# RMSNorm statistics issued chunk by chunk inside the projections, and the FFN-down split around the next tile's front

## What is computed

```
h = rmsnorm(x, g_pre1)
z = h @ w_in                    # 512 columns for S5, 256 for pooling, 256 memory queries
y_ssm = gelu(S5 scan(z[:512]));  y_ssm *= sigmoid(y_ssm @ w_glu + b_glu)
y_pool = per-group linear(trailing means 2/4/8/16 minus the frame)
y_mem = attention of 4 heads into 256 memory tokens
gates = sigmoid(h @ w_gate + b_gate)
merged = gates0*(y_ssm @ w_br_ssm) + gates1*(y_pool @ w_br_pool) + gates2*(y_mem @ w_br_mem)
x = x + rmsnorm(merged @ w_out, g_post1)
h2 = rmsnorm(x, g_pre2)
a, g = split(h2 @ w_ffn_up);  f = (gelu(causal depthwise conv3(a)) * g) @ w_ffn_down
x = x + rmsnorm(f, g_post2)
```

## Time and profile before

| | us |
|---|---|
| median of 2 runs (3299.61 and 3336.57) | 3318.09 |
| the profiled execution's own time | 3302.41 |
| span of its slowest core, core 6 | 3301.0 |
| spans of the 8 cores | 3282.2 to 3301.0 |
| TensorE (matmul) busy on core 6 | 1810.6 (55%) |
| TensorE weight loads | 1355.1 (41%) |
| VectorE busy | 1449.1 (44%) |
| ScalarE busy | 962.0 (29%) |
| GpSimd busy | 686.0 (21%) |

### The profile page before, as it was taken

One profiled execution on the slowest core, in us unless ns is written; L12 is line 12 of the kernel. 1 busy time (PEld: TensorE's weight loads), 2 busy tenths in 40 slices (PEclk: granted clock), 3 DMA queues, 4 the chain that ended last, 5 costly groups with the idle time before them and its releaser, 6 DMA issues.

```text
span 3301.0 us, 52796 instructions; the slowest of 8 cores (3282.2 to 3301.0 us)
## 1 busy us (share of the span) xinstructions
PE 1810.6 (55%) x16066; PEld 1355.1 (41%) x16066; DVE 1449.1 (44%) x2761; ACT 962.0 (29%) x2215; POOL 686.0 (21%) x2374
## 2 busy tenths in 40 slices
PE   0121345555555456676676676675676676675542
PEld 0121234334333334554554554554554454454432
DVE  3763266655655524334334334334244244235321
ACT  0000244344334223233233232233233233233232
POOL 2003400000000051241241241231332322322103
PEclk9999656656656667777778777778778778778655
DMA  9997312212211123343344344344344344344344
GB/s 112 111 109 121 102 58 77 77 56 73 77 64 65 58 71 128 117 158 140 123 140 141 126 144 146 127 136 155 133 137 150 117 154 142 108 144 153 115 173 151
DMA packets 101749, 387.12 MB, mean 117 GB/s; under 512 B 14144, under 2 KB 55744, under 8 KB 71872
## 3 DMA queue, kind: packets, MB, share of 16 engines
q1 hardware_dynamic: 98640, 351.77, 31.8%
q0 software_dynamic: 2832, 31.98, 8.6%
HBM read 406.47 MB, written 41.22 MB: 136 GB/s over the span
## 4 chain that ended last, share of the span: by engine, by line
PE 42%; DVE 24%; ACT 12%; issue 11%; POOL 6%; DMA 5%; DVEq 1%; ACTq 0%; POOLq 0%; SPq 0%
PE p_pm L331 36%; DVE s_hT L311 5%; ACT s_Zc L315 4%; DMA s_wsl<-wbf 4%; DVE s_xT L299 3%; DVE s_rstd L586 3%; PE p_pst L331 3%; ACT s_sq L327 3%; PE p_pt L334 3%; POOL s_Sall L299 2%; DVE s_tf L311 2%; DVE s_actT L299 2%; DVE s_rden L754 1%; DMA s_wstage<-wpool 1%; DVE s_m2T L299 1%
## 5 line engine op out<-in xcount | busy, mean ns | idle before, releaser
L331 PE MATMUL p_pm<-s_hT,s_wsl 128*128 128x256 bf16 (+1 forms) x6272 | 794.8, 292 | 462.3 <-DVE s_hT L311 350.4
L331 PEld LDWEIGHTS p_pm<-s_hT,s_wsl 128*128 128x128 bf16 x6272 | 618.0, 108 | 640.1 <-issue 514.5
L307 DVE TENSOR_SCALAR s_rstd<-p_pst 128x256 f32<-128x256 f32 (+1 forms) x61 | 25.0, 410 | 698.0 <-PE p_pst L331 698.0
L331 PE MATMUL p_pst<-s_sq,s_onesb 128*128 128x256 bf16 (+1 forms) x488 | 151.3, 333 | 302.4 <-ACT s_sq L327 299.5
L311 DVE SCALAR_TENSOR_TENSOR s_cbuf<-s_abuf,s_prm,s_cbuf 128x256 f32<-128x256 f32 (+1 forms) x396 | 182.7, 461 | 245.7 <-POOL s_cbuf L307 223.6
L319 POOL COPY s_abuf<-s_ahist 128x2 f32<-128x2 f32 x242 | 46.6, 193 | 1000.8 <-ACT s_abuf L315 990.6
L331 PEld LDWEIGHTS p_pst<-s_sq,s_onesb 128*128 128x128 bf16 x488 | 49.7, 102 | 399.8 <-issue 398.2
L331 PE MATMUL p_pm<-s_actT,s_wsl 128*128 128x256 bf16 (+1 forms) x1584 | 185.3, 282 | 30.7 <-DMA s_wsl<-wbf 21.6
L299 POOL TENSOR_TENSOR s_Sall<-s_Sall,s_ct 64x64 f32<-64x64 f32 x522 | 165.9, 318 | 75.4 <-POOL s_ct L299 0.4
L315 ACT COPY s_Zc<-p_pt 32x1024 bf16<-32x1024 bf16 (+1 forms) x132 | 132.3, 1002 | 163.6 <-PE p_pt L334 157.4
L331 PEld LDWEIGHTS p_pm<-s_actT,s_wsl 128*128 128x128 bf16 x1584 | 151.1, 105 | 63.1 <-issue 37.7
(11 more groups left out here) (136 smaller groups left out, 3086.0 us busy)
## 6 DMA issues: line engine op xcount, KB each, us to landing
s_wsl<-wbf SPq DMA_DIRECT2D x224, 1024.0 KB, 5.8
s_wsl<-wbf SPq DMA_DIRECT2D x72, 704.0 KB, 5.2
wbf<-wsrc POOLq DMA_DIRECT2D x23, 1024.0 KB, 136.8
s_wsl<-wbf SPq DMA_DIRECT2D x36, 512.0 KB, 5.0
s_xT<-xT_p SPq DMA_DIRECT2D x16, 1024.0 KB, 5.6
s_wstage<-xT_p SPq DMA_DIRECT2D x16, 1024.0 KB, 6.0
wbf<-wsrc POOLq DMA_DIRECT2D x8, 704.0 KB, 275.7
yT_p<-s_xT SPq DMA_DIRECT2D x4, 1024.0 KB, 5.4
```

What stands on the lines that cost most here:

```text
L307: e.tensor_scalar(out=out, in0=a, scalar1=s1, scalar2=s2, op0=op0, op1=op1))
L331: e.matmul(out, lhsT, rhs, start=start, stop=stop))
```

## The change

`norm_stats` is split into `stat_chunk` (one square and one matmul) and `stat_finish` (scale, root, reciprocal). Three things use the pieces. In `merge_out` and in `ffn_down` the statistics of a chunk of `m2T` are issued right behind its projection and copy. In `resid_norm` after `merge_out` the statistics of the new x are issued right behind the add of each chunk (`next_stats`), and `ffn_up` starts with `stat_finish`. And `drive` no longer runs the whole next `front` ahead of `ffn_down`: the order is now next front A1, FFN-down chunks 0 to 3, next front A2, FFN-down chunks 4 to 7 with the residual. The count of squares, statistics matmuls and projections is the same.

```diff
-    def norm_stats(src, srck, n):
-        for kc in range(8):
-            s_, sk = sqR.next()
-            act(s_[:, 0:n], src[:, kc, 0:n], AF.Square, [srck], [sk])
-            mm(pst[:, 0:n], onesb[:], s_[:, 0:n], kc == 0, kc == 7, ["onesb", sk], ["pst"])
+    def stat_chunk(src_ap, srck, kc, n):
+        s_, sk = sqR.next()
+        act(s_[:, 0:n], src_ap, AF.Square, [srck], [sk])
+        mm(pst[:, 0:n], onesb[:], s_[:, 0:n], kc == 0, kc == 7, ["onesb", sk], ["pst"])
+
+    def stat_finish(n):
         ts("dve", rstd[:, 0:n], pst[:, 0:n], 1.0 / D, EPS, ALU.mult, ALU.add, ["pst"], ["rstd"])
         act(rstd[:, 0:n], rstd[:, 0:n], AF.Sqrt, ["rstd"], ["rstd"])
         E("dve", ["rstd"], ["rstd"], lambda e, n=n: e.reciprocal(out=rstd[:, 0:n], in_=rstd[:, 0:n]))
+
+    def norm_stats(src, srck, n):
+        for kc in range(8):
+            stat_chunk(src[:, kc, 0:n], srck, kc, n)
+        stat_finish(n)
...
@@ merge_out, resid_norm, ffn_up
                 cp("act", m2T[:, ot, 0:n], p_[:, 0:n], [pk], ["m2T"])
-        resid_norm(n, P_GP1, xb, xk)
-
-    def resid_norm(n, gofs, xb, xk):
-        norm_stats(m2T, "m2T", n)
+                stat_chunk(m2T[:, ot, 0:n], "m2T", ot, n)
+        resid_norm(n, P_GP1, xb, xk, next_stats=True)
+
+    def resid_norm(n, gofs, xb, xk, next_stats=False):
+        stat_finish(n)
         for ot in range(8):
...
             tt("dve", xb[:, ot, 0:n], xb[:, ot, 0:n], f_[:, 0:n], ALU.add, [xk, fk], [xk])
+            if next_stats:
+                stat_chunk(xb[:, ot, 0:n], xk, ot, n)
 
     def ffn_up(segs, n, first_main, xb, xk):
-        norm_stats(xb, xk, n)
+        stat_finish(n)
         make_h(xb, xk, n, 1)
...
-    def ffn_down(n, xb, xk):
-        for ot in range(8):
+    def ffn_down(n, xb, xk, ots, fin):
+        for ot in ots:
...
             cp("act", m2T[:, ot, 0:n], p_[:, 0:n], [pk], ["m2T"])
-        resid_norm(n, P_GP2, xb, xk)
+            stat_chunk(m2T[:, ot, 0:n], "m2T", ot, n)
+        if fin:
+            resid_norm(n, P_GP2, xb, xk)
...
@@ drive
             back_a(d, nxt)
             if nxt is not None:
-                front(nxt)
-            back_b(d)
+                front(nxt, part="A1")
+            back_b(d, 0)
+            if nxt is not None:
+                front(nxt, part="A2")
+            back_b(d, 1)
```

More of the change, by code:

```diff
@@ L913, in back_a, with back_b @@
         ffn_up(segs, n, d["first_main"], xb, xk)
-    def back_b(d):
+    def back_b(d, half):
         n = d["n"]
         xb, xk = xbufs[d["par"]]
-        ffn_down(n, xb, xk)
+        if half == 0:
+            ffn_down(n, xb, xk, range(0, 4), False)
+            return
+        ffn_down(n, xb, xk, range(4, 8), True)
         for (dst_ap, c0, sn) in d["ydst"]:
```

## The result

The changed kernel takes 3409.38 us (median) against 3300.5 us of the kernel before: ratio 1.032, 95% interval 1.0285 to 1.0354. The medians lie 109 us apart, the spans of the two profiled executions 106.3 us (3301.0 to 3407.3); 3397 us were forecast. In some executions of any version the cores of a die ran at a lower granted clock and the time was some per cent longer: the ratios here leave out the executions in which this showed clearly, the medians do not.

A forecast was written before the change was run, and what follows sets the result against it. No engine is full: TensorE works in relay with the small engines, beside a GpSimd scan with 3.9 us of slack. Terms 98 - 18 + 41 + 12 - 27 - 11 + 1 = +96, unrounded +95, on 3302.4: 3397 us, range 3340 to 3430.

The forecast's parts named there:

- Part 1: Statistics inside `merge_out`: TensorE holds 1.17 us per chunk at clock 0.50; +12.3 us a tile, +98 us for 8 tiles.
- alternating: Rival, chance 0.12: the clock in `merge_out` runs half at either level, 22.5 us a tile, 3369 us in all.
- 1.00 throughout: Rival, chance 0.08: the clock stays at 1.00 throughout `merge_out`, giving 3340 us, +1.1%.
- The rival in which TensorE passes the waiting matmul: Rival, chance 0.04: no hold at the statistics matmuls; `merge_out` loses 3 us, 3228 us in all.
- Part 2: Second statistics inside the residual: adds every 1.09 us, but less work after the last; -2.3 us a tile, -18 us for 8.
- Part 3: Four FFN-down chunks ahead of the projections cover the 9.03 us wait but take 17.7 us; +5.8 us in seven tiles, +41.
- Ahead of the 40-token tile: Last, small tile: +12 us from FFN-down chunks before its projections, -11 us from the S5 front to `s5_back`.
- cold start: FFN-down chunks ahead of the projections start at clock 0.50, then rise; 2.3 us added to their time.
- The fourth rival: Rival, chance 0.04: FFN-down at clock 0.50 too, four chunks 24.7 us and projections starting cold; about 3481 us.
- Part 4: S5 front to `s5_back`: the scan needs 68.7 of 72.6 us, so only -3.9 us in seven tiles, -27 us.
- the 40-token tile itself: Work within the last, small tile: +1 us, since its small chunks wait for weights anyway.

The follow-up runs named there:

- Run 1: Changed kernel with the eight statistics matmuls of `merge_out` back in one row behind the eight projections: 3309.47 us, ratio 1.0027 to the kernel before.
- Run 3: Changed kernel with ten useless matmuls behind each `merge_out` projection in the full tiles, where TensorE stood idle: 3368.54 us, ratio 1.0193 to the kernel before.
- Run 6: Changed kernel with each statistics matmul issued behind the next chunk's projection, in `merge_out` and FFN-down: 3255.51 us, ratio 0.989 to the kernel before.
- Run 4: Changed kernel with a GpSimd scan of four operations a step instead of five: 3364.44 us, ratio 1.0163 to the kernel before.
- Run 5: Kernel before with only the scan cut to four operations a step instead of five: 3287.95 us, ratio 0.9957.
- Run 2: Kernel before with only the FFN-down split around the next front's A2, all statistics in rows at their old places: 3296.28 us, ratio 0.9976.

## Why the prediction was right

The forecast was 3397 us, +95 us on the terms below. In the profiled executions the span grew by 106.3 us (3301.0 to 3407.3). The sums over the tiles below are taken from the two timelines of TensorE.

**Part 1, `merge_out`:** +98 forecast, 209.33 - 109.50 = +99.8 measured. Wait 1.17 us, clock 0.50, 3.23 us a chunk (3.25 measured), 26.0 us (26.13). (The prediction's eight chunks of 3.23 us are 25.8, not the 26.0 that it sets.) Run 1 takes this part out and gives back 100 us. What the forecast used was the wait that the old kernel showed once, multiplied by eight, and the clock that the stretches with holes showed. Both clock rivals, alternating and 1.00 throughout, are excluded by the eight windows at 0.50. Run 3 shows that the clock is in fact a cause and that it is the holes that keep it from rising: fill them, and it rises. They need not bring it down once it is up: the FFN-down chunks behind the first keep 1.00 over holes of the same 1.17 us (11.60 us, 8.09 of them matmul). Those stretches differ in two things, the level at which they start and the length of the runs between the holes (2.56 us against 1.9); no run tells which of the two decides. Run 6 shows that the hold is one of queue order. That agrees with the Trainium skill ("TensorE: Matmul & The Clock Gate", Step-by-step: what each phase is for), by which matmuls stay in program order. The rival in which TensorE passes the waiting matmul is excluded by the 1.17 us behind every chunk.

**Part 2, second statistics:** -2.3 us a tile forecast. From the end of the first statistics to the end of the second it is 1802.84 to 1817.18, 14.3 us, against 16.4 before: -2.1. Over the eight full tiles it is -16.0 us, forecast -18. The step was 1.15 us instead of 1.09, since a single square takes 0.42 us (1810.52 to 1810.94); I had taken half of a pair's 0.72. The hand-over to the add at 1811.04 is the 0.1 that I took. This part was not tried alone.

**Part 3, chunks ahead of the projections:** +5.8 us a tile forecast, +4.8 in the tile shown (1882.55 to 1906.39 is 23.8 us against 19.05), +36.1 in the seven tiles (forecast +41). The first chunk came out of the slow clock sooner (3.65 us for 22 matmuls where my 2.3 us of cold start made 4.9). Ahead of the 40-token tile +11.0, forecast +12. The fourth rival, the FFN-down at 0.50 throughout, falls with the chunks of 2.56 us. One reading in the prediction is wrong, without harm to its sum: the clock did not fall in the wait of 9.03 us (from 1843.3 on) but before it, among the statistics matmuls of A1, between 1841 and 1842:

```profile
1841.00:1842.00 1.00, 0.65 (x3) 0.21 (x3) 0.00 (x0) 0.72 (x2) 0.00 (x0) 0.57 0.01 6
```

(The third number from the right is the clock.)

**Part 4, the scan as the new wait:** -3.9 us a tile forecast, (484.10 - 508.48) / 7 = -3.5 measured; the waiting for `Sbf` came out at 8.09 us in the tile shown and 7.5 on average in the seven, where about 7 was forecast. Ahead of the 40-token tile -10.3, forecast -11. Runs 4 and 5 show the mechanism: the same shorter scan is worth 61 us between profiled executions with the change and 14 without.

**The sum.** Added up over all tiles, the parts as measured give 99.8 - 16.0 + 36.1 + 11.0 - 24.4 - 10.3 = +96.3 us, and +97.7 with the 1.4 us of the 40-token tile itself. So the terms met the sum within 3 us, partly by luck: parts 1, 2 and 4 came out some 7 us above their forecasts, part 3 some 6 below. Of the other 8.6 us, which no term names, 2.7 lie before the first `merge_out`, and 5.1 lie in `ffn_up`, which starts slower in the tile shown (48 matmuls in 7.96 us instead of 7.04): its clock rises later. Why it rises later no run tests.

One sentence of part 3 and 4 hid a cost that the sum did not need, but the next kernel would: that the order of the loads "costs nothing as long as a chunk at 3.84 us and its neighbour cover a load". With the holds the condition held. Runs 2 and 6, without them, wait 2.4 and 2.3 us for weights in the tiles shown and 15.6 and 12.1 us in the seven: the holds had hidden it.

## What to carry to other kernels

TensorE, which works its matmuls off in order, paid at once for a matmul whose input another engine makes out of its last result: 1.17 us of hold for each. Interleave such a step one stage later, so that its input is made beside the next stage's work. Before moving work into a gap, look for the second chain beside the one that bounds (here 68.7 us of scan under 72.6 us of TensorE), since its slack is all that can be won there. And where holes are cut into a run of matmuls, price the matmuls at the low clock as well, if the run starts at it: here it stayed at 0.50 in all eight tiles, which was about half of the loss in `merge_out`, while in the FFN-down, with longer runs between the holes, it stayed at 1.00.

## What the hardware showed that I had not expected

Adding 640 useless matmuls made the kernel 41 us faster (run 3). The reading of `Sall` in swapped order on GpSimd (a step of -1 in the innermost axis) shows no cost beside the straight one: 0.31 us each for 64x64 in run 4. A half-width product takes 0.25 us, little less than the full-width 0.31. From the start of the first product to the start of what follows, two halves take 0.78 us and the whole 0.45 (1926.16 to 1926.94 in the changed kernel, 1903.04 to 1903.49 in run 4).
